# TensorE's order in an attention loop: the second branch's part of a unit in front of the scores three units on

## The reference, cut to what matters

```python
# A: window of 2 chunks of 64, grouped queries, one learned sink per head
scores = jnp.einsum('bnqkgd,bnskd->bnkgqs', qc, kb) * (HEAD_DIM ** -0.5)
m = jnp.maximum(jnp.max(scores, axis=-1, keepdims=True), sink)
p = jnp.exp(scores - m)
probs = p / (jnp.sum(p, axis=-1, keepdims=True) + jnp.exp(sink - m))
out = jnp.einsum('bnkgqs,bnskd->bnqkgd', probs, vb)
...
# B: own chunk and 8 before it, with a relative bias per head
scores = jnp.einsum('bnqhd,bnshd->bnhqs', qc, kb) * (HEAD_DIM ** -0.5) + bias
probs = jax.nn.softmax(scores, axis=-1)
out = jnp.einsum('bnhqs,bnshd->bnqhd', probs, vb)
```

## Time and profile before

| | |
|---|---|
| median of 3 runs | 2433.61 us (2433.05 to 2434.36) |
| the profiled execution | 2432.92 us, of it 2431.0 us span |
| mean granted TensorE clock | 0.97 |
| busy: TensorE, VectorE, ScalarE, GpSimd | 2287.4, 1299.0, 1028.8, 813.2 us |
| attention stage in the span | about 780 to 1093 us |

### The profile page before, as it was taken

The page is one execution under the profiler, slowest core; times in us unless marked ns, Lnnn a source line. Parts: engine busy times, 40 slices in busy tenths (PEclk is TensorE's granted clock), DMA queues, the critical chain, the costliest instruction groups (busy, mean ns, idle before and its releaser), DMA issues. The chain is left out here.

```text
span 2431.0 us, 36728 instructions
## 1 busy us (share of the span) xinstructions
PE 2287.4 (94%) x12226; PEld 1964.8 (81%) x12227; DVE 1299.0 (53%) x1939; ACT 1028.8 (42%) x1817; POOL 813.2 (33%) x782
## 2 busy tenths in 40 slices
PE   7999999999999999998999999499999999999990
PEld 6888888888887999887899998388888888888870
DVE  7112223211010888876433333877668578789885
ACT  6111112111112878873222211565456466667653
POOL 0355566540000111123222221245434444455450
PEclk8999999999999999999999999699999999999995
DMA  5356766641232776756554442699978889899987
GB/s 191 105 156 239 255 206 185 217 151 53 77 126 94 236 243 184 222 130 211 162 152 148 140 138 96 225 311 309 299 241 282 275 260 328 281 368 346 316 283 290
DMA packets 236537, 518.52 MB, mean 213 GB/s; under 512 B 24978, under 2 KB 91682, under 8 KB 235300
## 3 DMA queue, kind: packets, MB, share of 16 engines
q1 hardware_dynamic: 164020, 352.57, 41.9%
q0 software_dynamic: 30048, 86.79, 14.8%
q10 hardware_dynamic: 42384, 78.07, 8.9%
HBM read 385.64 MB, written 131.70 MB: 213 GB/s over the span
## 5 line engine op out<-in xcount | busy, mean ns | idle before, releaser
L468 DVE TENSOR_TENSOR pj_w_lo<-pj_w_raw,pj_w_hi 128x1024 fp32r<-128x1024 f32 x38 | 50.2, 1321 | 518.8 <-ACT pj_w_hi L343 518.8
L343 ACT ACTIVATE pj_w_hi<-pj_w_raw 128x1024 fp32r<-128x1024 f32 x38 | 40.2, 1059 | 529.6 <-PE pj_bank L562 477.4
L2315 POOL TENSOR_TENSOR ex_wd_lo<-weights_raw_d,ex_wd_hi 128x1024 fp32r<-128x1024 f32 x64 | 200.4, 3152 | 123.9 <-ACT ex_wd_hi L2217 120.0
L562 PE MATMUL pj_bank<-pj_hT_lo,pj_w_hi 128*128 128x512 f32 x864 | 230.9, 389 | 0.0
L562 PE MATMUL pj_bank<-pj_hT_hi,pj_w_hi 128*128 128x512 f32 x864 | 230.9, 389 | 0.0
L562 PE MATMUL pj_bank<-pj_hT_hi,pj_w_lo 128*128 128x512 f32 x864 | 230.9, 389 | 0.0
L562 PEld LDWEIGHTS pj_bank<-pj_hT_hi,pj_w_lo 128*128 128x128 f32 x864 | 162.2, 188 | 33.7
L562 PEld LDWEIGHTS pj_bank<-pj_hT_hi,pj_w_hi 128*128 128x128 f32 x864 | 162.2, 188 | 33.6
L562 PEld LDWEIGHTS pj_bank<-pj_hT_lo,pj_w_hi 128*128 128x128 f32 x864 | 162.2, 188 | 33.6
L2419 DVE TENSOR_TENSOR ex_wd_lo<-weights_raw_d,ex_wd_hi 128x1024 fp32r<-128x1024 f32 x64 | 162.1, 2571 | 4.0 <-ACT ex_wd_hi L2217 3.8
L1846 PE MATMUL mg_y_ps<-first_hi,mg_w_hi 128*128 128x256 f32 x512 | 149.2, 291 | 14.4 <-DVE mg_w_lo L1728 7.9
(11 more groups left out here) (333 smaller groups left out, 5819.5 us busy)
## 6 DMA issues: line engine op xcount, KB each, us to landing
weights_raw_g<-in_w_exp_gate_dram SPq DMA_DIRECT2D x128, 512.0 KB, 6.7
weights_raw_u<-in_w_exp_up_dram SPq DMA_DIRECT2D x128, 512.0 KB, 9.1
weights_raw_d<-in_w_exp_down_dram SPq DMA_DIRECT2D x128, 512.0 KB, 7.2
pj_w_raw<-in_w_feat_dram SPq DMA_DIRECT2D x38, 512.0 KB, 4.8
scratch_gates<-pj_f_hi ACTq DMA_DIRECT2D x32, 512.0 KB, 5.0
mg_g_in<-scratch_gates SPq DMA_DIRECT2D x120, 128.0 KB, 2.8
pj_x_in<-in_x_dram SPq DMA_DIRECT2D x16, 512.0 KB, 3.9
scratch_qk<-pj_f_hi ACTq DMA_DIRECT2D x16, 512.0 KB, 5.0
```

Of the source, the lines that this page charges most:

```text
L343: act.activation(w_hi[n % 2][:], w_raw[n % 2][:], ACT.Copy).then_inc(whi_done, 1)
L468: dve.tensor_tensor(w_lo[n % 2][:], w_raw[n % 2][:], w_hi[n % 2][:], ALU.subtract).then_inc(wlo_done, 1)
L562: last = pe.matmul(eight[4 * p + b][:], w[p][:, k * P:(k + 1) * P], h[:, k, b * NB:(b + 1) * NB], start=(k == 0 and n == 0), stop=(k == KD ...
L2315: pool.tensor_tensor(wd_lo[p][:, j, :], raw.buffer[2][j][:], wd_hi[p][:, j, :], ALU.subtract).then_inc(d_lo_pool, 1)
```

## The change

In the loop of TensorE the call of `scores(u + 3)` moves from before branch A's four calls to behind them. Nothing else differs.

```diff
                 if 2 <= u < B_UNITS + 2:
                     (values_shared, values_alone)[u % 2](u // 2 - 1)
-                if u + 3 < B_UNITS:
-                    scores(u + 3)
                 if 0 <= u - V_START < V_BATCHES:
                     a_turn_v(u - V_START)
                 s = a_step(u, 5)
...
                 s = a_step(u, 0)
                 if s is not None:
                     a_scores(s)
+                if u + 3 < B_UNITS:
+                    scores(u + 3)
             pe.wait_ge(sink_done, 1)
```

## The result

| | before | changed |
|---|---|---|
| median | 2433.33 us (2431.62 to 2434.36, 4 runs) | 2449.41 us (2448.30 to 2450.75, 4 runs) |
| span of the profiled execution | 2431.0 us | 2448.8 us |
| ratio | | 1.0067, 95% interval 1.0054 to 1.0079 |

The sign and the place were right. The loss of 16.1 us is about twice the 8.3 that the sum gave. It lies above the forecast of +5 to +15 and at the price of rival 3 (2449 or more), and only 0.6 us inside the range, whose upper end was set by that rival and not by the sum. That the range holds it is in part luck.

A forecast was written before the change was run, and what follows sets the result against it. TensorE, busy for 94% of the span, was taken to bound the kernel, with VectorE and ScalarE nearly full in the attention stage. Terms +4.7 and +3.6 made +8.3 us, added to the median for 2441.9 us; range 2435.0 to 2450.0.

The forecast's parts named there:

- rival 3: The clock falls in units 6 to 12, or late scores also delay the exponentials: 2449 us or more; chance 0.10.
- First part: Units 3 to 10, V's eight pieces: scores, `biased`, split and turn form a loop of 2.88 us a unit; +4.7 us.
- (a): Ten sink steps 3 units apart: their scores wait longer for VectorE's `apt_lo`; 0.64 us each, 6.4 in ten.
- (b): Sink steps 4 apart, third unit odd: values wait up to 0.46 us longer for `pt_lo`, about a dozen places; 0 to +5.5.
- (c): Where scores wait and a piece of branch A follows, the piece fills the wait; gain of at most 4.9 us.
- The walk: Every start moved through units 26 to 48: +0.7 us in 22 units, 5.2 such stretches, +3.6 us for the sink steps.
- The clock: No term in the sum: the clock was expected to stay at 1.00 despite the new idle time in V's units.
- the second part: The 32 sink steps, units 12 to 131: two costs and one gain taken together, +3.6 us.

## Why the prediction was right in sign and half in size

**First part, V's pieces: right.** The loop was predicted at 2.88 us and is 2.82; the term was +4.7, the marks give +4.7, and the run that changes V's pieces alone gives +4.4 to +5.3.

**(a), the ten near steps: right in mechanism, too small.** The term was 0.64 us each. Measured: from 2.1 to 10.5 us, 0.84 each. I took unit 26 as the pattern, where VectorE had a backlog and its times did not move. In the three units 70, 103 and 114 it has none: it waits for the scores itself (0.33, 0.89 and 0.59 us). There TensorE goes from its last scores to the step's scores in 3.0 to 3.1 us, the length of the chain, and what its other work doesn't fill of it is the wait: 1.4 to 1.7 us.

**(b), the values: too large.** Up to 0.46 us in a dozen places was the bound; measured is a growth from 2.3 to 3.6 us in all, the part that the trace puts to the engine's issue included, so +1.3.

**(c), the gain: right in its bound.** The waits before the scores fell by 3.9 of 4.9 us. That a filled wait mostly moves to the next unit was the weaker half of the argument: 1.0 us in 3 places is all that is left or new (1.7 in 5 in the second profile).

**The walk: the sum of these came out too low.** It gave +3.6; the waits measure +5.8. It stretched units 26 to 48, with two of the ten steps and none of the three long ones, over the whole stage. Its parts, times 5.2, were about +6.2 for (a), +3 for (b) and -5.7 for (c), the filled waits less the new ones; measured are +8.4, +1.3 and -3.9. Its filled waits alone, 1.7 us in 22 units, come to 8.8 us over the stage, more than the 4.9 that the earlier trace rows has to give: the sample was not typical, and that could have been seen. The errors of (b) and (c) nearly cancel, which is luck.

**The clock: this step failed.** The sum had no term for it. I had weighed the new waits of the first part only, where the clock indeed stayed at 1.00, and placed rival 3's fall there, with a chance of 0.10. The measured time is rival 3's, but the falls came in other units, those of the second part, behind waits that term (a) had made long: 5.1 us in the profiled execution, the largest part of what was missing. The Trainium skill ("TensorE: Matmul & The Clock Gate", section "Why this matters for your kernels") advises against idle gaps of TensorE between bursts of matmuls, but it names longer ones than any wait before these falls. So its advice did not foretell these falls either, and the measurement decides: waits of 1.4 to 1.7 us can be enough, and the same wait is not enough each time.

**The end of the stage: not in the sum.** +1.5 us in the first profile. In the second profile of the changed kernel the same stretch, from unit 124 to the merge, takes 23.2 us, as before the change (23.3). So this part differs from execution to execution and is not shown to come from the change; the slow clock of the earlier trace rows lies there in both kernels, at other places.

**What stays open** is the price of the clock in the timings. The profile says 5.1 us. If the parts simply add, it is less: the ten near steps alone (+9.4, no fall) and all the others alone (-1.4, no fall) make +8.0 between units 13 and 124, and all steps in front, with three falls, make +10.6, so 2.6 for the falls. In the timings, taking back the three steps with falls gave back 3.7 us in all, of which 3.5 are waits, and the run with ten exchanges and a clean clock is timed like the one with three falls. Either a slow TensorE lets VectorE catch up and part of the loss returns, or falls appear elsewhere in other executions. The runs don't separate the two.

## What to carry over

Before moving an engine's work in front of a step that others wait for, look up what the moved work itself waits for, and where that stands in the other engine's queue: if it is behind the answer to the very step that is now last, the exchange closes a loop. Move only in the units where the trace shows a wait that the moved work can fill: twelve chosen exchanges took 4.4 us of waits away and gained about 2.6 us (an interval that just touches none), where 90 cost 16. And take the pattern for a sum from the unit with the least slack, not from the first one that shows the effect; when a sample is stretched over a stage, hold each of its parts against the stage's own total.

## What was unexpected of the hardware

The clock fell to 0.50 behind waits of 1.37, 1.71 and 1.51 us in one execution; in another of the same program one of the three had no fall and one fall lasted 7 us instead of 3.4; the eight waits of 0.8 to 1.1 us in its V units and near steps had none. Over all profiles, between units 3 and 124, 9 of the 15 waits of 1.37 us and more had a fall within about 2 us behind their end, and 6 had none; no fall came in the eight profiles whose longest wait was 1.27 us or less. Idle time of VectorE proved a poor witness: 25.7 us of waiting for scores, against 7.7, cost nothing that could be measured.
